# TensorE's stage products cut into steps of half the length, in a kernel that lives on row gathers

## The reference, cut to what matters

```
x = x + mixer(rmsnorm(x))
q = rmsnorm(x) @ w_q                       # 1024 x 2048: 8 heads of 2 x 128
s = q . sub_keys                           # 128 scores per half head
idx, gate = best 16 pairs of each head     # 128 rows per token
a = u[idx] . h ; w = gate * gelu(a)        # rows of 1024 from a table of 16384
x = x + sum_k w_k * v[idx_k]
x = x + sigmoid(rmsnorm(x) @ w_g) * (p @ w_p)
```

## Time and profile before

| | us |
|---|---|
| median of 3 runs | 2930.66 (2930.23 to 2931.85) |
| the profiled execution | 2932.58 |
| its span, first to last instruction | 2930.8 |
| PE busy in the span | 2277.9 |
| DVE busy | 2134.5 |
| ACT busy | 1075.1 |
| POOL busy | 1274.9 |

### The profile page before, as it was taken

The page is one execution under the profiler, slowest core; times in us unless marked ns, Lnnn a source line. Parts: engine busy times, 40 slices in busy tenths (PEclk is TensorE's granted clock), DMA queues, the critical chain, the costliest instruction groups (busy, mean ns, idle before and its releaser), DMA issues.

```text
span 2930.8 us, 23774 instructions
## 1 busy us (share of the span) xinstructions
PE 2277.9 (78%) x6832; PEld 1225.8 (42%) x6832; DVE 2134.5 (73%) x4435; ACT 1075.1 (37%) x3179; POOL 1274.9 (44%) x1028
## 2 busy tenths in 40 slices
PE   4797757976879997889687998799867797765555
PEld 3454224622445653455254565346524353231113
DVE  4685867885697766767979776685795887687774
ACT  1343333433233432733333434363332344333222
POOL 0353443445434444444443344454443344455551
PEclk7899889999999998999899999899988999987777
DMA  4999999999999999999999999999999999999993
GB/s 192 421 387 421 420 420 420 399 420 421 420 389 416 410 421 421 419 421 420 399 421 394 420 418 421 420 418 414 421 387 421 419 379 404 420 419 421 420 420 162
DMA packets 164932, 1178.02 MB, mean 402 GB/s; under 512 B 18496, under 2 KB 19904, under 8 KB 23488
## 3 DMA queue, kind: packets, MB, share of 16 engines
q0 software_dynamic: 147456, 1073.81, 89.1%
q1 hardware_dynamic: 16768, 100.59, 8.3%
q10 hardware_dynamic: 576, 2.10, 0.2%
HBM read 1174.32 MB, written 2.10 MB: 401 GB/s over the span
## 4 chain that ended last, share of the span: by engine, by line
PE 35%; DMA 34%; DVE 20%; ACT 5%; issue 4%; POOL 2%; SPq 0%; DVEq 0%; ACTq 0%; POOLq 0%
DMA slot<-in_uv,idx 34%; PE acc L838 18%; DVE slot L1433 7%; PE M L559 4%; PE B L559 3%; DVE X L1426 3%; PE B L631 2%; POOL slot L536 2%; PE M L631 1%; ACT diag L1034 1%; ACT w L1028 1%; PE B L722 1%; PE M L722 1%; DVE top_u L1116 1%; DVE SD L1111 1%
## 5 line engine op out<-in xcount | busy, mean ns | idle before, releaser
L838 PE MATMUL acc<-slot,diag 128*128 128x512 f32 x2908 | 1559.1, 677 | 602.2 <-ACT diag L1034 601.2
L536 POOL DMA_INDIRECT slot<-in_uv,idx x1024 | 1274.7, 1245 | 1599.9 <-PE acc L838 1113.7
L1433 DVE CUSTOM_DVE_ANT_0 slot<-slot,HP 128x1024 f32<-128x1024 f32 x1024 | 1245.9, 1222 | 631.5 <-DMA slot<-in_uv,idx 622.2
L838 PEld LDWEIGHTS acc<-slot,diag 128*128 128x128 f32 x2908 | 576.5, 211 | 1432.0 <-ACT diag L1034 877.7
L1026 ACT ACTIVATE act_a<-a 128x1 f32<-128x1 f32 x1024 | 206.8, 202 | 1627.7 <-DVE a L1433 1626.6
L1426 DVE SCALAR_TENSOR_TENSOR X<-slot,w,X 128x1024 f32<-128x1024 f32 x297 | 380.7, 1282 | 16.3 <-ACT w L1028 16.1
L1028 ACT ACTIVATE w<-act_a,gate 128x1 f32<-128x1 f32 x1024 | 301.6, 295 | 33.3
L1034 ACT ACTIVATE diag<-cst,w 128x128 f32<-128x128 f32 x727 | 291.9, 402 | 23.8
L559 PE MATMUL M<-w,TT 128*128 128x256 f32 x400 | 90.6, 380 | 0.0
L559 PE MATMUL B<-w,TT 128*128 128x256 f32 x400 | 90.6, 380 | 0.0
L631 PE MATMUL M<-TT,w 128*128 128x256 f32 (+1 forms) x448 | 87.4, 350 | 0.0
(11 more groups left out here) (171 smaller groups left out, 1489.0 us busy)
## 6 DMA issues: line engine op xcount, KB each, us to landing
w<-in_wq SPq DMA_DIRECT2D x28, 1024.0 KB, 9.1
slot<-in_uv,idx POOLq DMA_INDIRECT x1024, 14.4
w<-in_ple_wg SPq DMA_DIRECT2D x8, 1024.0 KB, 9.0
w<-in_w_o SPq DMA_DIRECT2D x8, 1024.0 KB, 9.0
w<-in_w_dq SPq DMA_DIRECT2D x6, 1024.0 KB, 9.6
w<-in_w_uq_nope SPq DMA_DIRECT2D x8, 768.0 KB, 8.4
w<-in_ple_wp SPq DMA_DIRECT2D x5, 1024.0 KB, 9.0
slot<-in_wq SPq DMA_DIRECT2D x4, 1024.0 KB, 10.2
```

The lines of the kernel that those rows point to most:

```text
L536: nc.gpsimd.indirect_dma_start(out=slot[s][:], out_offset=None, in_=uv[g // NC], in_offset=bass.IndirectOffsetOnAxis(ap=idx[:, g % HPB, k: ...
L838: last = nc.tensor.matmul(acc[:, half * 512:half * 512 + 512], diag[adds_on_pe(n) % DIAGS][:], slot[s][:, D + half * 512:D + half * 512 + ...
L1433: nc.vector.tensor_tensor_reduce(out=slot[s][:, 0:D], in0=slot[s][:, 0:D], in1=HP[:, g % HPB, :], scale=1.0, scalar=0.0, op0=ALU.mult, op1 ...
```

## The change

PE's products of a stage are cut in four steps where there were two. In `products` the step ends after half of the k blocks of each block of tokens; with one block of tokens there are now two steps where there was one. In asks this is done with n = 2 alone (with n = 1, DB // n is DB and the two steps stay). uq, keys and add are cut likewise. No product, addition, load or wait is added or dropped, and no engine but PE has another program.

```
@@ products
-                        if ch:
-                            yield STEP
-                        last = product(MB[ch][:, at(i):at(i) + cols], lhsT, ch, wp, kb, cols)
+                        for k in range(kb):
+                            if (ch or k) and k % (kb // 2) == 0:
+                                yield STEP
+                            last = nc.tensor.matmul(MB[ch][:, at(i):at(i) + cols], lhsT[:, k, ch * P:(ch + 1) * P],
+                                                    wp[:, k * cols:(k + 1) * cols],
+                                                    start=(k == 0), stop=(k == kb - 1))
                     last.then_inc(weights_used, 1)
@@ asks_stage, queries
-                        if e:
-                            yield STEP
                         for k in range(DB):
+                            if (e or k) and k % (DB // n) == 0:
+                                yield STEP
@@ keys_stage
-                    if h == H // 2:
+                    if h and h % 2 == 0:
                         yield STEP
...
                     for half in range(2):
+                        if half:
+                            yield STEP
@@ uq_stage
                         for k in range(QR // P):
+                            if k == QR // P // 2:
+                                yield STEP
@@ add_stage
-                    if i:
-                        yield STEP
                     for half in range(2):
+                        if i or half:
+                            yield STEP
```

## The result

The changed kernel takes 2965.84 us (median of 4 runs, 2962.58 to 2971.06) against 2931.26 us before (4 runs, 2930.23 to 2936.06): the ratio is 1.0116, 95% interval 1.0098 to 1.0135. It is 1.2% slower, 34.6 us, where 2.7 us were forecast, and outside the range. The profiled execution took 2965.97 us, its span is 2964.2 us.

The account below looks back on a forecast made before the run. The DMA engines were taken to bound the kernel, so only their idle time counts. Slots -1.9, add +3.0 and scores +1.6 gave +2.7 us, 2935.3 on the profiled execution, a median of 2933.4 us; range 2921 to 2946.

Parts of the forecast that it names:

- What bounds the kernel: Whole kernel: its end moves only with the DMA engines' idle time; 21 windows of 277 together lack 17.9 us.
- Item 1: Windows where PE is full: additions come sooner and free slots earlier, -1.9 us, bounds 0 and -3.7.
- Item 2: Add stage, groups 2, 4 and 6: ends one PE addition later and DVE waits, +3.0 us, bounds 0 and +5.2.
- Item 3: Asks, two blocks: scores end later, DVE waits but mostly catches up in gaps; +1.6 us, bounds 0 and +15.5.
- The sign that I had named for the slower rival: Windows at 850 or 2160 us, behind asks: a DMA share clearly lower than before.
- the slower rival: Three asks stages: DVE's waits for scores are not made up, costing 15.5 us; 2944.3 us, chance 0.20.
- Item 4: Keys, values and queries: ACT waits 1.72 or 3.44 us more each, covered by the reserve; 0, bounds 0 and +15.
- Item 5: Weight loads, shortest for uq's third piece: buffers free later, loads still in time; 0, bounds 0 and +1 per group.
- Item 6: Neighbouring parts, three or four places: three steps fall together, 5.2 us without an addition; 0, bounds 0 and +1.
- Item 7: PE in full stretches: granted clock stays at 2.4 GHz, no new gaps between its own steps; 0.
- the clock rival: PE's cut products: clock falls between shorter bursts, one in five at 1.2 GHz, 48 us of PE; 2947, chance 0.04.
- the likeliest case: Whole kernel: the forecast itself, median 2933.4 us, chance 0.62, spreading from 2927 to 2938 by the bounds.

Follow-up runs that it names:

- half steps with ends kept: Against the kernel before: products in half steps, except that all an engine waits for keeps two steps, scores at their old place; 2930.66 us, 0.9991.
- asks alone and the scores put back: Against the kernel before: only the queries of asks in four steps, scores with the third quarter of the next queries; 2926.80 us, 0.9986.

## Why the prediction was wrong

- *What bounds the kernel* held. The time moved with the idle time of the DMA engines, and it came mostly from windows behind asks and add.
- *Item 1, slots free earlier (-1.9)*: right in kind. The windows at 530 and 2440 us filled up, and half steps with ends kept show no loss against before. With asks alone and the scores put back it was 5 us faster (interval 0 to 8), where the sooner scores may have their part.
- *Item 2, add (+3.0)*: the size fits the stage alone (+4, DVE's wait longer by 1.72 us). In the whole change the wait was 6.68 us, since I priced each handover by the additions that pass ahead of its own end. The handover before it, from the last gates product to ACT's sigmoids, stands in no item, so it was put at nothing. The additions that went ahead had been the stock that hid it.
- *Item 3, scores (+1.6)*: this is the step that failed. "DVE has gaps in which it catches up" was read from a trace in which DVE waited 2 us. The waits became 7.55, 3.58 and 3.66 us in group 5 instead of about 5.5, 3 and at most 1.7, PE lost time in turn, and the stage lost 10.4 us there. In all DVE waited 53.1 us for scores, where I had named 25 to 40. The sign that I had named for the slower rival showed at 850 us, where the DMA share fell from 0.77 to 0.59. Asks alone cost 15 us; the bound of 15.5 us that I gave it was its size, and the slower rival was right for this stage.
- *Item 4, ACT (0)*: wrong for attention, which cost 15 us, the bound. I took the waits for keys, values and queries and set a reserve of 14 us against them. That reserve was still there in the changed kernel (landings of 12.2 to 17.1 us from 1010 to 1040 us), but it didn't last: from 1040 to 1070 us landings go down to 6.5 us, where they had been 10.4 and more, and the window at 1060 us has a DMA share of 0.90 instead of 1.01. I also left out ACT's wait for dq's product, which grew from 0.18 to 6.17 us in group 2 and from 2.27 to 6.27 us in group 4, and the last wait for uq grew by 5.6 us in group 2 (4.85 to 10.42), not by 3.44. For the queries of asks, where ACT's waits doubled, 0 was right.
- *Item 5, weights*: nearly right. PE waited once for a load of uq's weights, 0.2 us, and its weight loads twice, 1.9 us in all. *Item 6*, lumps, was not tried by itself.
- *Item 7, the clock*: the mean granted clock of the profiled executions went from 0.905 to 0.900, but the four runs of the changed kernel read 0.900 to 0.907 and those of the kernel before 0.896 to 0.910, so this shows no difference. Additions after a gap took 3.59 us, so part of a handover's price is paid at 1.2 GHz, but the clock rival as I put it, falling between shorter bursts, is refuted: half steps with the ends kept show no loss against before. By the Trainium skill, page "TensorE: Matmul & The Clock Gate", section "Loop structure matters more than you think", it is waits between bursts that let the clock fall; the trace agrees in part, as here it fell behind PE's gaps of 2.59 and 2.18 us, not between products and additions, while in another kernel it did not fall behind a gap of 2.59 us (last section).
- The range was built from bounds of single items, while the likeliest case set three of them near their lower ends for one kind of reason, that lateness is made up, by DVE's gaps or by the reserve. If that reason falls, all fall together: 1.9 us given back, and up to 3 + 15.5 + 15 us lost, is 2962, close to what came. Part of this closeness is luck, as the handovers of gates and dq are in no item.

Open: why the gathers' packets took 12 us more in sum, how much of the whole loss is PE's idle time and how much its clock, what the last gates piece costs by itself, and which of the attention stages weighs most.

## What to carry to other kernels

When work is cut finer and interleaved, look first at who waits for its end: a finer step moves the end of a part, and an in-order queue passes that on to everything behind it. Count what is left behind the end, for that stock is what hides the handover. A reserve read from the trace before holds only as long as the waits stay as short as they are there, so terms that lean on the same reserve belong in one rival, not in separate small sums.

## What the runs showed of the hardware

An addition whose record reads 1.88 us at 2.4 GHz took 3.59 us after PE had idled 2.59 us at 921 us and 2.18 us at 2130 us, with a granted clock of 0.52 in both stretches. But in the kernel with gates and add cut, a gap of 2.59 us was followed by one of 1.98 us at a granted clock of 1.00. The same length of gap does not always end at 1.2 GHz. And the packets of the same gathers took 2623 us in sum where they had taken 2611. Over the profiles of all 14 kernels this sum goes from 2608 us in the one with the shortest span (2924.2 us) to 2628 in the one with the longest (2982.8).
